# Eight of sixteen attention rounds over a paged cache moved into the prompt's heads, on keys that the host lays out turned

## What is computed

```
def sample_attention(q_lat, q_pe, ckv_new, kpe_new, cache_ckv, cache_kpe, page_table):
    ...
    def one(args):
        ql, qp, cn, kn, pages = args
        cp = cache_ckv[pages].reshape(-1, KV_LORA)
        kp = cache_kpe[pages].reshape(-1, QK_ROPE_DIM)
        s_past = (jnp.einsum('thl,pl->htp', ql, cp) + jnp.einsum('thr,pr->htp', qp, kp)).astype(jnp.float32) * ATTN_SCALE
        ...
        p = jax.nn.softmax(jnp.concatenate([s_past, s_new], axis=-1), axis=-1).astype(cp.dtype)
        return jnp.einsum('htp,pl->thl', p[..., :n_past], cp) + jnp.einsum('hts,sl->thl', p[..., n_past:], cn)
```

## Time and profile before

| | us |
|---|---|
| median of 3 runs | 1349.68 (1349.44 to 1350.97) |
| the profiled execution's own time | 1349.55 |
| its span, first to last record | 1347.8 |
| PE busy | 1325.2 |
| DVE, POOL, ACT busy | 801.8, 686.6, 591.0 |

### The profile page before, as it was taken

How to read it: one execution, slowest core, us unless ns; L and a number is a source line. 1 busy time by engine, 2 the same in 40 slices (tenths; PEclk the granted TensorE clock), 3 DMA queues, 4 the chain that set the end, 5 groups by cost and what they waited for, 6 DMA issues and landing times.

```text
span 1347.8 us, 28262 instructions
## 1 busy us (share of the span) xinstructions
PE 1325.2 (98%) x11262; PEld 1247.4 (93%) x11262; DVE 801.8 (59%) x1230; ACT 591.0 (44%) x1005; POOL 686.6 (51%) x467
## 2 busy tenths in 40 slices
PE   6999999999999999999999999999999999999997
PEld 6877599999999999999999977779999999999997
DVE  6688867655454544667566656665675545454534
ACT  5112356443434343435666554442454434343432
POOL 2322344488888886434332132211348878787731
PEclk9999999999999999999999999999999999999999
DMA  6654412333333334524321399861223222332221
GB/s 241 168 176 127 134 65 90 110 109 109 109 110 109 109 109 122 195 72 117 84 71 62 112 334 315 312 245 33 94 65 98 93 94 93 97 92 96 93 95 67
DMA packets 147299, 169.30 MB, mean 126 GB/s; under 512 B 44576, under 2 KB 130848, under 8 KB 141920
## 3 DMA queue, kind: packets, MB, share of 16 engines
q1 hardware_dynamic: 142176, 133.38, 31.9%
q0 software_dynamic: 4608, 33.56, 6.8%
q10 hardware_dynamic: 384, 0.55, 0.2%
HBM read 154.68 MB, written 12.42 MB: 124 GB/s over the span
## 4 chain that ended last, share of the span: by engine, by line
PE 92%; SPq 3%; DVE 2%; ACT 1%; issue 1%; DMA 1%; POOL 0%; DVEq 0%; ACTq 0%
PE ps L1775 30%; PE ps L1911 21%; PE ps L1899 19%; PE ps L2042 4%; PE ps L1813 3%; PE ps L2096 2%; PE ps L2140 2%; SPq L534 2%; SPq L533 1%; PE ps L2215 1%; PE ps L1826 1%; PE ps L2086 1%; PE ps L2131 1%; PE ps L2150 0%; PE ps L2157 0%
## 5 line engine op out<-in xcount | busy, mean ns | idle before, releaser
L641 POOL TENSOR_TENSOR wl<-raw,wh 128x512 fp32r<-128x512 f32 (+2 forms) x249 | 430.3, 1730 | 431.9 <-ACT wh L768 431.8
L768 ACT ACTIVATE wh<-raw 128x512 fp32r<-128x512 f32 (+2 forms) x253 | 192.4, 762 | 361.4 <-PE ps L1775 189.6
L1775 PE MATMUL ps<-xh,wh 128*128 128x272 f32 x704 | 148.7, 293 | 10.5 <-DVE xl L1150 10.3
L1911 PE MATMUL ps<-mh,wl 128*128 128x272 f32 x768 | 158.8, 288 | 0.0
L1911 PE MATMUL ps<-mh,wh 128*128 128x272 f32 x768 | 158.4, 288 | 0.0
L1911 PE MATMUL ps<-ml,wh 128*128 128x272 f32 x768 | 158.4, 288 | 0.0
L641 POOL TENSOR_TENSOR wl<-wuv,wh 128x512 fp32r<-128x512 f32 x104 | 133.8, 1298 | 43.7 <-ACT wh L768 43.7
L1775 PE MATMUL ps<-xl,wh 128*128 128x272 f32 x704 | 146.5, 290 | 0.0
L1775 PE MATMUL ps<-xh,wl 128*128 128x272 f32 x704 | 146.3, 289 | 0.0
L1775 PEld LDWEIGHTS ps<-xh,wh 128*128 128x128 f32 x704 | 111.8, 191 | 15.4 <-POOL wl L641 10.3
L1911 PEld LDWEIGHTS ps<-mh,wh 128*128 128x128 f32 x768 | 120.6, 188 | 0.0
(11 more groups left out here) (317 smaller groups left out, 2922.2 us busy)
## 6 DMA issues: line engine op xcount, KB each, us to landing
raw<-w_up SPq DMA_DIRECT2D x32, 1024.0 KB, 5.3
raw<-w_down SPq DMA_DIRECT2D x32, 1024.0 KB, 5.0
raw<-w_pw SPq DMA_DIRECT2D x11, 1024.0 KB, 5.5
kp_seq<-cache_kpeT SPq DMA_DIRECT2D x256, 32.0 KB, 2.2
kp<-kp_seq SPq DMA_DIRECT2D x32, 256.0 KB, 4.4
shifted<-ext SPq DMA_DIRECT2D x96, 66.5 KB, 2.0
raw<-w_o SPq DMA_DIRECT2D x4, 1024.0 KB, 5.0
raw<-w_dq SPq DMA_DIRECT2D x3, 1024.0 KB, 5.9
```

The source lines that it names most:

```text
L641: pf.tensor_tensor(weight(wl, u), weight_raw(u), f32(weight(wh, u)), ALU.subtract).then_inc(w_lo, 1)
L768: af.activation(weight(wh, u), weight_raw(u), ACT.Copy).then_inc(w_hi, 1)
L1775: m = tf.matmul(ps[:, bank_of(u) + bank, 0:width], w[:, k, :], a[:, k, part], start=(k == 0 and n == 0), stop=(k == nk - 1 and n == 2))
L1911: m = tf.matmul(acc_of(u)[:, h, :], w[:, k, :], a[:, k0 + k, h * HALF:(h + 1) * HALF], start=(k0 == 0 and k == 0 and n == 0), stop=(k0 > 0 ...
```

## The change

The host lays the latents of the cache out turned too (`cache_kT`: a page is five pieces of 128 rows by 64 numbers, one rotary and four latent ones). For the first 16 chunks (rounds 0 to 7) SP copies all five pieces of a page within DRAM and loads 1 MB of turned latents per chunk into `raw` (the place where the weight blocks came), besides the 256 KB of rotary keys; no transposes are made for them. POOL gathers the same chunks as before for the values. Rounds 8 to 15 stay as they were. The queries' products of all heads stand in one row ahead of head 0; their results take the place of the layer's input x, which is saved to DRAM (`x_keep`, 2.2 MB) and read back in two parts. Head h then holds round h: its rotary and latent scores behind the prompt's scores, `values(h - 1)` behind `turned(h)`, `probs_turned(h)` at the end. Six pages stand ahead of a weight load, from one block earlier.

```
-EARLY_PAGES, LATE_PAGES = 5, 9
+EARLY_PAGES, LATE_PAGES = 6, 8
...
+TURNED = 2 * NH
+NAT_SLOT = [j % 4 if j < TURNED else (4, 0, 1, 5, 6, 2, 3)[(j - TURNED) % CB] for j in range(NCH)]
+KEY_SLOT = [j % 2 if j < TURNED else (2, 3, 4, 5, 6, 0, 1)[(j - TURNED) % CB] for j in range(NCH)]
+PIECES = 1 + 2 * KC
...
+    for n in range(NH // 2):
+        units.append(Unit("qr", n, QC, block("qr", n, QC, P), 0))
+        b = block("uq", 2 * n, QC, 2 * P)
+        units.extend([Unit("uq", 2 * n + e, QC, b, e * P) for e in range(2)])
...
+                j, w = n // PPC, PAGE // 2
+                np_ = PIECES if j < TURNED else 1
+                sp.dma_start(k_pages[j, :, 0:np_, n % PPC * w:(n % PPC + 1) * w],
+                             cache_kT[bass.ds(page, 1), :, 0:np_, :].rearrange("n p e c -> (n p) e c")).then_inc(k_seq[b], 16)
...
+            def turned_keys(j):
+                if j < 2:
+                    sp.wait_ge(w_lo, PROJ[NH - 1] + 1)
+                else:
+                    sp.wait_ge(ks_mm, j // 2)
+                sp.wait_ge(k_seq[j // CPS], 16 * PAGES)
+                sp.dma_start(f32(raw[:, j % 2, :]), k_pages[j, :, 1:PIECES, :].rearrange("p e c -> p (e c)")).then_inc(t_keys[j % 2], 16)
 
...
+                    sp.dma_start(x_keep, x[:, :, :]).then_inc(x_kept, 16)
...
+            for h in range(1, NH):
+                low(UK[h])
+                if (h + 1) // 2 < NH // 2:
+                    low(UV[(h + 1) // 2][(h + 1) % 2])
+                if h > 1:
+                    for k in range(2):
+                        pool.wait_ge(t_keys[k], 16 * (h + 1))
+                    gather(2 * h)
+                    gather(2 * h + 1)
+            pool.wait_ge(w_lo, UK[NH - 1] + 1)
+            gather(TURNED)
+            gather(TURNED + 1)
+            gather(TURNED + 2)
+            pool.wait_ge(pv_mm, NH)
+            for j in range(TURNED + 3, NCH):
+                gather(j)
...
+                cached_max(h)
+                if h > SPB and h % SPB == 1:
+                    weighted_sum(h // SPB - 1)
+                if h + 1 < NH:
+                    keys_low(h + 1)
+                    if h // 2 + 1 < NH // 2:
+                        values_low(h // 2 + 1, h % 2)
+                else:
+                    keys(NH, (1,))
+                if h > 0:
+                    dve.wait_ge(ks_exp, h + 1)
+                    values_out(h - 1)
+                if h % SPB == SPB - 1:
+                    collect(h // SPB)
+                    differences(h // SPB)
+                elif h > 0:
+                    spread_weights(h // SPB - 1)
+                pvh_()
+                df.tensor_tensor(ml[:, h, 0:NP], ps[:, 7, :], f32(mh[:, h, 0:NP]), ALU.subtract).then_inc(pv_lo, 1)
+                if h == 0:
                     dve.wait_ge(ko_mm, 1)
-                    df.tensor_copy(onew[:, :, :].rearrange("p a b -> p (a b)"), ps[:, 6, :]).then_inc(ko_out, 1)
-                if i > SPB and i % SPB == 1:
+                    df.tensor_copy(onew[:, :, :].rearrange("p a b -> p (a b)"), ps[:, 3, :]).then_inc(ko_out, 1)
+                if h % SPB == SPB - 1:
+                    weights(h // SPB)
...
+            product(PROJ[1], xh, xl)
+            for n in range(1, NH // 2):
+                product(QR[n], xh, xl)
+                product(PROJ[2 * n], xh, xl)
+                product(PROJ[2 * n + 1], xh, xl)
...
+            def turned_scores(i):
+                b = i // SPB
+                rotary_scores(i)
+                for s in range(SETS):
+                    j = 2 * i + s // 2
+                    if s % 2 == 0:
+                        pe.wait_ge(t_keys[j % 2], 16 * (i + 1))
+                    for c in range(KC):
+                        for par in range(2):
+                            m = tf.matmul(scores_at(i, par)[NS * s:NS * (s + 1)].rearrange("p (q g s) -> p q g s", q=2, s=ROWS), qs[:, c, b, :],
+                                          page_order(turned_latents(j, par, c), s), start=False, stop=(c == KC - 1))
+                m.then_inc(ks_mm, 1)
...
+            for h in range(NH):
+                scores(h)
+                if h == 0:
+                    pe.wait_ge(kcopy, 2 + 4 * NH // 2 + KC)
+                    pe.wait_ge(freed, units[UV[0][1]].done)
+                turned_scores(h)
+                if h == 0:
+                    scores_new()
+                turned(h)
+                if h > 0:
+                    values(h - 1)
+                if h + 1 < NH:
+                    keys_product(h + 1)
+                    if h // 2 + 1 < NH // 2:
+                        values_product(h // 2 + 1, h % 2)
+                else:
+                    keys(NH, range(2))
+                if h == 0:
+                    probs_new()
+                outputs(h)
+                if h == 0:
+                    values_new()
+                if h > SPB and h % SPB == 1:
+                    pe.wait_ge(ko_out, h + 1)
+                    folded(h // SPB - 1)
+                probs_turned(h)
+            keys(NH, (2,))
             pe.wait_ge(pv_lo, NH)
-            keys(0, range(3, 6))
-            probs_new()
-            keys(0, range(6, 8))
-            for i in range(NSC):
...
+    def turn(cache, c):
+        keys = n(cache).reshape(-1, ROWS, RPC // 2, 2, c, n(cache).shape[-1] // c)
+        keys = keys.transpose(0, 3, 5, 4, 2, 1) if c == 1 else keys.transpose(0, 5, 3, 4, 2, 1)
+        return keys.reshape(keys.shape[0], P, -1, PAGE // 2)
```

More of the change, by code:

```diff
@@ L308, in decoder_program @@
+        kp2 = sb("kp2", [P, CB - 2, RPC * ROPE], F32, smp_mem)
         smp_mem.close()
@@ L413, in bank_of @@
         def bank_of(u):
+            if units[u].kind in ("uk", "uv") and units[u].n > 0:
+                return units[u].out % 2
             return 4 if u == 2 else 2 * (units[u].out % 2)
@@ L772, in ahead @@
                 for n in FOLLOW.get(u, ()):
-                    high(n)
+                    if not u < U_WO <= n:
+                        high(n)
             def split_hi(dst, a, scale=1.0):
@@ new lines, in new_exp, with new_probs_out @@
+            def new_exp():
+                act.wait_ge(n_max, 2)
+                af.activation(nmxn[:, :], stn[:, :, 0], ACT.Copy, scale=-SCALE).then_inc(act_at, 1)
+                own()
+                for n in range(2):
+                    af.activation(sn[:, n, :], sn[:, n, :], ACT.Exp, bias=nmxn[:, n:n + 1], scale=SCALE,
+                                  accum_out=stn[:, n, 1:2]).then_inc(n_exp, 1)
+            def new_probs_out():
+                act.wait_ge(n_pt, 1)
+                af.activation(pn[:, :, :].rearrange("p a b -> p (a b)"), ps[0:NS, 3, 0:2 * P], ACT.Copy).then_inc(n_out, 1)
@@ new lines, in _ @@
+            act.wait_ge(s_out, 64)
+            for h in range(NH):
+                softmax()
+                for g in range(3):
+                    pt_()
+                    af.activation(pth[:, TGROUPS[g]], ps[:, 4 + g, 0:TGROUPS[g].stop - TGROUPS[g].start], ACT.Copy).then_inc(pt_hi, 1)
+                if h + 1 < NH:
+                    keys_high(h + 1)
+                    ahead(UK[h + 1])
+                else:
+                    keys(NH, (0,))
+                cached_exp(h)
+                if h == 0:
+                    new_exp()
+                if h + 1 < NH:
+                    if h // 2 + 1 < NH // 2:
+                        values_high(h // 2 + 1, h % 2)
+                if h == 0:
+                    new_probs_out()
+                pv_()
+                af.activation(mh[:, h, 0:NP], ps[:, 7, :], ACT.Copy).then_inc(pv_hi, 1)
+                if h % SPB == SPB - 1:
+                    weights_out(h // SPB)
+                if h > SPB and h % SPB == 1:
+                    folded_out(h // SPB - 1)
+                probs_out(h)
@@ L1087, in _ @@
+            keys(NH, (2, 4, 6))
+            for i in range(NH, NSC):
+                cached_exp(i)
                 keys(i + 1, (0, 2, 4))
-                if i > SPB and i % SPB == 1:
+                if i % SPB == 1:
                     folded_out(i // SPB - 1)
@@ L1692, in _ @@
+            keys(NH, (3, 5, 7))
+            for i in range(NH, NSC):
+                cached_max(i)
+                if i % SPB == 1:
                     weighted_sum(i // SPB - 1)
                 keys(i + 1, (1, 3, 5, 7))
-                if i > 0:
-                    values_out(i - 1)
+                values_out(i - 1)
                 if i % SPB == SPB - 1:
                     collect(i // SPB)
+                    differences(i // SPB)
                     weights(i // SPB)
-                elif i > 0:
+                else:
@@ L2054, in _ @@
             product(PROJ[0], xh, xl)
+            product(PROJ[1], xh, xl)
+            for n in range(1, NH // 2):
+                product(QR[n], xh, xl)
+                product(PROJ[2 * n], xh, xl)
+                product(PROJ[2 * n + 1], xh, xl)
             values_product(0, 1)
+            queries_s()
             pe.wait_ge(root, 6)
```

(16 more changed lines are left out.)

416 lines of the change are left out of this document (222 added, 194 removed).

## The result

The median went from 1349.79 us to **1356.73 us** (6 runs, 1353.69 to 1358.36); the ratio is 1.0047, interval 1.0035 to 1.0059. The kernel is slower by half a per cent, where 1331 was forecast. The profiled execution took 1353.77 with a span of 1352.0, 4.2 us more than the one before, so the spans show 4.2 of the 6.9. But the two profiled executions differ already ahead of the change: the MLP stage of layer 0 begins in the chain of the kernel before and of the changed kernel at

What follows compares the result with a forecast made beforehand. PE was taken to bound the kernel, busy 1325 of 1348 us. The terms -29.2 - 2.5 + 1.4 + 0 + 6.3 + 3.9 + 1.8 gave -18.3, so 1331 us, range 1325 to 1339 (with rivals 1325 to 1354).

Steps and rivals of the forecast that it cites:

- The turned scores: 0: Latent scores in the heads: passes overlap across column tiles despite the new loop order, block stays 1.86 us, costing 0.
- the second rival: Turned scores: passes overtake, but not far enough; half the tiles abreast, block 4.0 us, time 1342; chance 0.08.
- Removed, -29.2: Eight cached rounds lose their key transposes on PE, 8 x (3.21 + 0.44) us: -29.2 us.
- First wait and row of products, -2.5 + 1.4: First scores' DVE wait and heads' idle PE go, -2.5 us; back-to-back queries' products wait for weights and splits, +1.4.
- Waits in the heads, +6.3: Turned probabilities wait for the softmax, now less covered: 0.9 us in each of 7 heads, +6.3 us.
- the first rival: Turned scores: tiles go one after another, block 6.7 us, covering the softmax waits; time 1364; chance 0.15.
- Head 0 and the folded sums, +3.9: Head 0's new exponents come 1.5 us late; folded sums in heads 3, 5, 7 wait 0.8 each: +3.9 us.
- The seam, +1.8: Between heads and round 8: keys wait for the gather of chunk 17, whose place comes free late, +1.8 us.
- Moved at no price: Queries' products and eight rounds' scores, values and turned probabilities take PE the same time; saving x costs nothing.
- Page copies, 0: MLP stage: six page copies and a weight load per 11.3 us block fit the DMA engines, costing 0.
- Rival 3: Transfers bound the heads: 4.72 MB takes 16.4 us at 288 GB/s, +11 us, time 1342; chance 0.08.

Runs made afterwards that it cites:

- experiment 3: Changed kernel with the turned scores in runs of six passes on a column tile, then two more on each; 1352.16 us (one run).
- experiment 10: Four tries at the seam of the tile-reordered changed kernel: later weight loads; later round-8 keys with seam edits; both; both with values first; 1348.17, 1343.0, 1346.03, 1341.08 us.
- experiment 1: Changed kernel with the loop over the four column tiles innermost in the turned scores; 1344.16 us, ratio 0.9964.
- experiment 5: Changed kernel with chunk 16 gathered ahead of 14 and 15, and round 8's rotary keys in places free earlier; 1351.18 us.
- experiment 8: Changed kernel with inner tile loop, turned-key loads from chunk 2 on cut to a quarter (wrong keys): 1345.14 us; with values ahead of turns too: 1335.61 us.
- experiment 9: Changed kernel with inner tile loop, chunks 16 to 20 bringing 256 KB instead of 1 MB (wrong results); 1340.46 us.
- Experiment 7: Changed kernel with inner tile loop and values(h - 1) ahead of turned(h); 1343.4 us.
- experiment 10's first try: Changed kernel with inner tile loop, the first two weight blocks of the output product loaded later; 1348.17 us (10 runs).

## Why the prediction was wrong

**The step that failed** is "The turned scores: 0". It took "the full effect, 1.86 us", and said itself that the rows didn't tell how far a pass goes past a waiting one. The block took 4.53 us: 8 x 2.67 = +21.4. The end weighed against it, strict order at 6.7, was wrong as well; the second rival's mechanism ("it overtakes, but not far enough", 4.0 us) was the right one, with a chance of 0.08, though its time, 1342, wasn't. What the runs put in its place: runs of 2, 4, 6 and 8 passes on a tile took 1.86, 1.96, 3.23 and 4.53 us. If a column tile holds one running and three waiting passes, and the list is dealt out in order and stops where the wanted tile is full, these are 8 x 0.216 plus three small steps for 2 and 4 (all fit), and plus three times 2 or 4 steps of 0.216 for 6 and 8: 1.8, 1.8, 3.0 and 4.3. The mechanism is fitted on 8 and 2, and foretold 6; 4 ruled out the single window, and the start times of the passes in experiment 3 show the second tile beginning just when three passes of the first are left waiting, in runs of six and of eight. That the thing is a queue for each tile is an inference from these lengths and starts.

This step alone doesn't give the sign. By the prediction's own sum a block of 4.53 us gives -18.3 + 21.4 - 6.3 = -3.2, so 1346, still a gain and inside its range; it had put the turning point at a block of about 5 us. It took the seam's miss too, and two smaller ones, to make the kernel slower.

The Trainium skill, TensorE: Matmul & The Clock Gate, Part 3: Packing small matmuls, says that matmuls start and end in strict program order. By it the four lengths would be near 3.9, 5.8, 5.8 and 6.7 (an estimate with steps of 0.23, 32 less one for each change of tile); the traces show them all shorter, 1.86, 1.96, 3.23 and 4.53. In one thing it pointed the right way: the order of the list matters.

**Removed, -29.2:** right. Against the kernel before, PE's list has 256 transposes less, at the same durations in the rounds that kept them.

**First wait and row of products, -2.5 + 1.4 = -1.1:** off by 2. From the MLP's start to the first scores the kernel before takes 658.84 - 267.73 = 391.1 us, the changed one 706.63 - 265.08 = 441.6. Ten products (45.9) and the samples' queries (3.54 in the trace of before) account for 49.4 of the 50.4: +1.0. The starts stand in the earlier trace rows and in the chains above. The wait of 1.34 us isn't gone: it stands as 1.30 ahead of the samples' queries (L2157), which need the same row sums from DVE (the traces of experiment 10 name DVE as what ended it). That the sums are long made by then was the wrong reading.

**Waits in the heads, +6.3:** none came, since the long block covered them, as the first rival said. In experiment 1 they are 6.8 in seven heads, 0.7 of it in head 0, which the forecast left out, and so 6.1 in six of the seven that it counted: the mechanism and the size were right, for the head that was forecast.

**Head 0 and the folded sums, +3.9:** 1.3 (for the new exponents) and 0.5. The folded sums wait once, not three times: what stands beside them covers more than was reckoned.

**The seam, +1.8:** the second failure, by size. It counted one gather. Measured: 3.19 + 0.64 + 0.96 + 1.85 + 1.07 = 7.7 us of idle PE, and 1.0 + 0.7 in the two blocks at lower clock (2.84 and 2.44 us in the chain, for 1.86 and 1.73): 9.4. What was missed: POOL's list puts chunk 16 behind two gathers that wait for turned keys, and PE's list puts its keys ahead of head 7's outputs, for which in turn the places of the next gathers and the rotary keys are held. The kernel before gathered its first seven chunks from 764 on, at the end of heads that left the DMA two thirds free (0.32); now seven start between 828 and 845 (the first four in POOL's rows above), beside the last turned keys and the rotary keys of the rounds behind, at a DMA share of 0.91. How much of the 7.7 us is late issue and how much the length of the transfers, experiments 5, 8, 9 and 10 don't settle: 5 and 9 speak for some of each, and the edits against late issue brought at most 1.2 us over experiment 1 once the tile order was good.

**Moved at no price:** nearly. In the heads the values take 1.86 for 1.73, the turns 1.24 for 1.09, the keys' product 1.59 for 1.40, together 3.5 us over the heads. Why wasn't tested; each of these blocks now stands at a change between column tiles and the full array.

**Page copies, 0:** right. The MLP blocks are 22.6 us a pair in both, at a DMA that carries up to 191 GB/s there.

**The sum** by measured terms, -29.2 + 21.4 + 1.0 + 1.8 + 9.4 + 3.5 = +7.9, against 6.85 from the MLP's start on; the 1.1 us between stay unassigned. The changed kernel's six runs scatter by 4.7 us, the four slower ones at a mean clock of 0.994 or 0.995 against 0.996 and 0.997. A mean clock lower by 0.002 to 0.003 over 1355 us is worth 2.7 to 4.1 us (an estimate), which is about the gap between the four and the two. That the lower clock comes from longer waits at the seam is likely by the one profile, and wasn't tested.

**Rival 3** (transfers bound the heads) didn't decide here, but it is the next bound, by the reason it gave: only two places, and a load that starts when the scores that read its place are done. Experiment 7 has 15.8 us a head, near its 16.4 at 288 GB/s flat. That is part of why the repairs together end at 1341 and not at the 1331 that was forecast; even with three quarters of the turned keys left out the time was 1335.6, and the seam (4.5 us of waits for gathers in that run), the row of products (+1.0) and the moved work (+3.5) are in the rest.

## What to carry to other kernels

When small matmuls share PE's array by column tiles, let the tile index be the inner loop, and count passes, not matmuls: here up to four on a tile in a row were nearly free (0.1 us), six cost 1.4 us and eight 2.7 on a block of 1.9. A row of the profile proves overlap only for the order in which it was taken; a price at nothing that rests on a longer reach than the row shows is a bound, and belongs beside the likeliest value. When work is moved into a quiet stretch, ask what prefetch lived in that stretch: its transfers come due where both stages meet. And a profile taken from the quickest of ten runs can't explain a median that lies almost 7 us above it (experiment 10's first try).

## What was not expected of the hardware

- The four block lengths above. A group's mean per matmul (382 ns) doesn't change with the order; only the group's busy time tells (36.8 against 15.6 us).
- A wait at the seam costs more than itself: with 5.8 us of idle PE the clock is 0.77 over the 15 us of experiment 9's rows, with 3.8 us 0.89. The eight transposes behind the 5.8 us took 1.97 us, where they take 1.09 behind the changed kernel's 3.19, and L2223 took 2.84 us for 1.86 in the changed kernel's stretch at 0.91.
- A gather of 1 MB, 7.9 us to landing in the earlier trace rows, took 10.3 in the changed kernel (median; 8.7 to 11.7), and 256 KB of rotary keys, 4.4 us in the page of the kernel before, 7.3 to 14.0 where PE waited for them.
- Turns of 128 columns behind a block on column tiles took 1.24 us for ten, against 1.09 behind full-width matmuls.
